# A sample's output projection and a router's logits on four column quarters of TensorE

## The reference

```python
def merge_branches(y_lru, o_nsa, ga, gb, w_proj_a, w_proj_b, w_out):
    return (sigmoid(ga) * (y_lru @ w_proj_a) + sigmoid(gb) * (o_nsa @ w_proj_b)) @ w_out

x = x + merge_branches(...)              # the residual
t = rms_norm(x, g_ffn)
logits = t @ router_w + router_b         # 1024 x 32
top_v, top_e = top_k(logits, 4)          # 4 of 32 experts for each row
gate = softmax(top_v)
# each expert: clamped SwiGLU of width 1024, its output weighted by gate and added to x
```

## Time and profile before

| | |
|---|---|
| three runs | 1765.46, 1769.73, 1770.02 us; median 1769.73 |
| profiled execution | 1770.05 us, its span 1768.40 us |
| TensorE's mean granted clock | 0.981 of full speed |
| busy in the span | PE 1694.9 us (96%), DVE 1137.3 (64%), ACT 886.6 (50%), POOL 220.2 (12%) |
| chain that ended last | PE 79%, DMA 11%, DVE 4%, issue 2%, ACT 2% |
| HBM | 488.10 MB read, 25.35 MB written, 290 GB/s over the span |

### The profile page before, as it was taken

How to read it: one execution, slowest core, us unless ns; L and a number is a source line. 1 busy time by engine, 2 the same in 40 slices (tenths; PEclk the granted TensorE clock), 3 DMA queues, 4 the chain that set the end, 5 groups by cost and what they waited for, 6 DMA issues and landing times.

```text
span 1768.4 us, 27559 instructions
## 1 busy us (share of the span) xinstructions
PE 1694.9 (96%) x10018; PEld 1312.8 (74%) x10018; DVE 1137.3 (64%) x1550; ACT 886.6 (50%) x1006; POOL 220.2 (12%) x262
## 2 busy tenths in 40 slices
PE   7999999999999999999989999999999999999998
PEld 4899978797776778777758675876768585876755
DVE  6766786645345756948668493848668493848661
ACT  5235645533322344737456472727466472727461
POOL 0022010003303123200100100100100100100100
PEclk9999999999999999999999999999999999999999
DMA  5063243114317617999999999999999999999995
GB/s 223 25 215 119 84 103 92 59 61 131 110 34 216 226 38 270 359 369 411 400 399 384 397 404 398 390 385 409 386 405 394 396 397 401 397 391 409 388 400 207
DMA packets 107795, 498.76 MB, mean 282 GB/s; under 512 B 20770, under 2 KB 41354, under 8 KB 57264
## 3 DMA queue, kind: packets, MB, share of 16 engines
q1 hardware_dynamic: 86592, 454.20, 65.5%
q0 software_dynamic: 20976, 42.93, 9.1%
q10 hardware_dynamic: 144, 0.55, 0.1%
HBM read 488.10 MB, written 25.35 MB: 290 GB/s over the span
## 4 chain that ended last, share of the span: by engine, by line
PE 79%; DMA 11%; DVE 4%; issue 2%; ACT 2%; SPq 0%; ACTq 0%; POOL 0%; DVEq 0%; POOLq 0%
PE bank L1247 23%; PE bank L1265 13%; DMA ring<-in_w_exp 10%; PE bank L751 7%; PE bank L803 5%; PE bank L651 5%; PE bank L1316 4%; PE bank L1301 3%; PE bank L678 3%; PE bank L1050 3%; PE bank L1025 1%; PE bank L837 1%; PE bank L816 1%; DMA slab<-in_w_tok 1%; PE bank L1218 1%
## 5 line engine op out<-in xcount | busy, mean ns | idle before, releaser
L2477 DVE TENSOR_TENSOR ring_rounded<-ring,wide_rounded 128x2048 fp32r<-128x2048 f32 x126 | 283.7, 2284 | 22.2 <-ACT wide_rounded L1719 22.1
L1719 ACT ACTIVATE wide_rounded<-ring 128x2048 fp32r<-128x2048 f32 x126 | 236.7, 1912 | 70.8 <-DMA ring<-in_w_exp 54.4
L1247 PE MATMUL bank<-ring_rounded,slab_rounded 128*128 128x512 f32 x672 | 261.7, 389 | 0.0
L2477 DVE TENSOR_TENSOR ring_rounded<-ring,xn_rounded 128x2048 fp32r<-128x2048 f32 x84 | 189.5, 2284 | 49.5 <-ACT xn_rounded L1719 49.1
L1247 PE MATMUL bank<-xn_rounded,slab_rounded 128*128 128x512 f32 x672 | 220.6, 399 | 0.0
L1719 ACT ACTIVATE xn_rounded<-ring 128x2048 fp32r<-128x2048 f32 x84 | 159.5, 1909 | 77.6 <-DMA ring<-in_w_exp 76.6
L1265 PE MATMUL bank<-wide_rounded,slab_rounded 128*128 128x512 f32 x504 | 170.6, 399 | 0.4 <-DVE slab_rounded L2571 0.3
L2617 DVE TENSOR_SCALAR slab<-bank 128x256 f32<-128x256 f32 x22 | 9.3, 425 | 238.0 <-PE bank L1301 238.0
L1247 PE MATMUL bank<-wide_rounded,slab_rounded 128*128 128x512 f32 x504 | 159.0, 390 | 0.0
L1301 PE MATMUL bank<-ring,slab 128*64 128x256 f32 x1408 | 156.2, 380 | 0.0
L751 PE MATMUL bank<-ring_rounded 128*128 128x260 f32 x768 | 149.4, 293 | 2.3 <-DVE slab_rounded L2092 2.3
(11 more groups left out here) (519 smaller groups left out, 3047.1 us busy)
## 6 DMA issues: line engine op xcount, KB each, us to landing
ring<-in_w_exp SPq DMA_DIRECT2D x384, 1024.0 KB, 12.8
ring<-in_w_blk SPq DMA_DIRECT2D x40, 512.0 KB, 3.7
slab<-in_w_tok SPq DMA_DIRECT2D x4, 1304.0 KB, 15.2
ring<-in_w SPq DMA_DIRECT2D x8, 512.0 KB, 3.2
ring<-in_w_out SPq DMA_DIRECT2D x2, 2048.0 KB, 14.9
xn<-in_xT SPq DMA_DIRECT2D x4, 520.0 KB, 8.2
ring<-in_k_cmp SPq DMA_DIRECT2D x32, 64.0 KB, 3.5
ring<-in_k_cmp POOLq DMA_DIRECT2D x32, 64.0 KB, 2.6
```

Of the source, the lines that this page charges most:

```text
L1247: r = mm(bank[:, c, :], a[:, 4 * h + k, :], w[:, k, :], start=False, stop=h == 1 and k == 3 and x == 2)
L1719: fn(WH[(2 * c + h) % 6], ring[:, half_of(c, h)], ACT.Copy).then_inc(S["wh_ready"], 1)
L2477: v.tensor_tensor(ring_r[:, half_of(c, h)], ring[:, half_of(c, h)], WHf[(2 * c + h) % 6], ALU.subtract)\
```

## The change

Tile 0's output projection is no longer three fp32r products of 512 columns, but f32: m's sample columns (a copy, `m_sample`, that ScalarE makes behind each high part) are stationary, 8 columns wide, and w_out, as WOH plus WOL, each read as f32, moves in four pieces of 256 columns, each written to its own 32 partitions of bank 3. These are 64 f32 calls for 48 fp32r matmuls. VectorE's residual of tile 0 goes in four pieces of 256 columns. The logits turn around: the router's 32 columns are stationary and the turned rows move, block pair j on partitions 32j to 32j + 31 of bank 3, 8 calls; ScalarE copies the 128 x 128 result (four partial sums, turned) to SBUF, and one f32 call with it as stationary operand and `stacked`, four unit matrices of 32 on top of each other, as moving operand adds the four and turns them back. That call stands in the middle of `out_part(t, 1, 0)`. VectorE builds `stacked` in three additions ahead of its preparation for the router. After the last tile, the second half of `first_expert(RT - 2)` moves between the two steps of the logits.

```diff
+        WOLf = [x.bitcast(F32) for x in WOL]
+        m_sample = kT_st[:, 1484:1484 + KD * NSA].rearrange("p (k n) -> p k n", k=KD)
+        logit_parts = oT_st[:, 1024:1024 + P]
+        stacked = oT_st[:, 1152:1152 + NE]
@@ tensor
-            def out_part(t, h, j):
+            def out_part(t, h, j, meanwhile=None):
                 n = tile_rows(t)[1]
-                if t == 0:
-                    pe.wait_ge(S["blk_lo"], NBLK + 8 + 2 * h + j + 1)
-                elif j == 0:
+                if t > 1 and j == 0:
                     pe.wait_ge(S["xm_ready"], 2 * t + h - 1)
                 for k in range(4 * j, 4 * j + 4):
-                    if t == 0 and h == 0:
+                    if t == 1 and h == 0:
                         pe.wait_ge(S["xw_lo"], 3 * KD + k + 1)
                     for x in range(3):
                         r = out_product(...)
+                    if meanwhile is not None and k == 4 * j + 1:
+                        logits(meanwhile)
+            def sample_rows():
+                for k in range(KD):
+                    pe.wait_ge(S["xw_hi"], 3 * KD + k + 1)
+                    for x in range(2):
+                        for j in range(4):
+                            h, a = j // 2, 256 * (j % 2)
+                            if k == 0 and a == 0:
+                                pe.wait_ge(S["blk_lo"], NBLK + 8 + 2 * h + 2)
+                            w = (WOHf, WOLf)[x][h].rearrange("p (k n) -> p k n", k=KD)
+                            r = mm(bank[32 * j:32 * j + NSA, 3, 0:256], m_sample[:, k, :], w[:, k, a:a + 256],
+                                   start=k == 0 and x == 0, stop=k == KD - 1 and x == 1)
+                            if k == KD - 1 and x == 1 and a:
+                                r.then_inc(S["wo_done"], 1)
...
+            def logits_by_expert(t):
+                n = tile_rows(t)[1]
+                pe.wait_ge(S["t_copied"], 3 * t + 2)
+                for x in range(2):
+                    for j in range(4):
+                        r = mm(bank[NE * j:NE * (j + 1), 3, 0:n], rwt[:, 2 * j + x, :], tT[:, 2 * j + x, 0:n], start=x == 0, stop=x == 1)
+                r.then_inc(S["lg_done"], 1)
+
             def logits(t):
                 n = tile_rows(t)[1]
-                pe.wait_ge(S["t_copied"], 2 * t + 2)
+                pe.wait_ge(S["t_copied"], 3 * t + 3)
...
-                for k in range(KD):
-                    r = mm(out, tT[:, k, 0:n], rwt[:, k, :], start=k == 0, stop=k == KD - 1)
-                r.then_inc(S["lg_done"], 1)
+                mm(out, logit_parts[:, 0:n], stacked, start=True, stop=True).then_inc(S["lg_done"], 1)
...
-            out_part(0, 0, 0)
-            out_part(0, 0, 1)
-            out_part(0, 1, 0)
-            out_part(0, 1, 1)
+            sample_rows()
             pe.wait_ge(S["m_ready"], 3 * KD)
             turn_part(0, 0)
...
-                logits(t - 1)
-                out_part(t, 1, 0)
+                logits_by_expert(t - 1)
+                out_part(t, 1, 0, t - 1)
...
             first_expert(RT - 2, range(0, 4))
+            logits_by_expert(RT - 1)
+            first_expert(RT - 2, range(4, KD))
             logits(RT - 1)
             places_before(RT - 1)
             places(RT - 1)
-            first_expert(RT - 2, range(4, KD))
             first_expert(RT - 1)
@@ scalar
             def merged_high(m):
                 act.wait_ge(S["m_ready"], 2 * KD + m + 1)
-                fn(MH[m], mT[:, m, :], ACT.Copy).then_inc(S["xw_hi"], 1)
+                fn(MH[m], mT[:, m, :], ACT.Copy)
+                fn(m_sample[:, m, :], mT[:, m, NPR:NT], ACT.Copy).then_inc(S["xw_hi"], 1)
...
+            def logits_copied(t):
+                n = tile_rows(t)[1]
+                act.wait_ge(S["lg_done"], 2 * t + 1)
+                fn(logit_parts[:, 0:n], bank[:, 3, 0:n], ACT.Copy).then_inc(S["t_copied"], 1)
...
             for t in range(RT):
                 if t >= 1:
                     turned_part(t - 1, 1)
+                    logits_copied(t - 1)
                 row_squares(t, 0)
@@ vector
             merged_low(KD - 1)
+            one(v.tensor_tensor(stacked, ident[:, 0:NE], ident[:, NE:2 * NE], ALU.add))
+            one(v.tensor_tensor(stacked, stacked, ident[:, 2 * NE:3 * NE], ALU.add))
+            one(v.tensor_tensor(stacked, stacked, ident[:, 3 * NE:4 * NE], ALU.add))
...
             def residual(t, h):
...
+                if t == 0:
+                    for j in (2 * h, 2 * h + 1):
+                        a = slice(256 * j, 256 * j + 256)
+                        one(v.scalar_tensor_tensor(xm[0:n, 0, a], bank[32 * j:32 * j + n, 3, 0:256], 0.5, xr[0:n, 0, a], ALU.mult, ALU.add),
+                            S["xm_ready"] if j % 2 else None)
+                    return
```

More of the change, by code:

```diff
@@ L1069, in turn_part @@
                 if t >= 1:
-                    pe.wait_ge(S["t_copied"], 2 * t + h - 1)
+                    pe.wait_ge(S["t_copied"], 3 * t + h - 2)
                 for k in range(4):
@@ L1691, in turned_part @@
                 if t >= 1:
-                    act.wait_ge(S["lg_done"], t)
+                    act.wait_ge(S["lg_done"], 2 * t - 1)
                 fn(tT[:, 4 * h:4 * h + 4, 0:n], bank[:, 2 + h, :].rearrange("p (k t) -> p k t", k=4)[:, :, 0:n], ACT.Copy)\
                     .then_inc(S["t_copied"], 1)
+            def logits_copied(t):
+                n = tile_rows(t)[1]
+                act.wait_ge(S["lg_done"], 2 * t + 1)
+                fn(logit_parts[:, 0:n], bank[:, 3, 0:n], ACT.Copy).then_inc(S["t_copied"], 1)
             def row_squares(t, h):
@@ L1748, in _ @@
                     high_half(0, 0, t - 2)
+            logits_copied(RT - 1)
             act.wait_ge(S["t_ready"], RT)
@@ L1848, in pair @@
                 block_of(n + 1, 1, "few", after_few=True)
-            act.wait_ge(S["lg_done"], RT)
+            act.wait_ge(S["lg_done"], 2 * RT)
             turned_rows(0)
@@ L2412, in choose @@
                 N = slice(0, n)
-                dve.wait_ge(S["lg_done"], t + 1)
+                dve.wait_ge(S["lg_done"], 2 * t + 2)
                 out = bank[N, 0, 0:NE] if t == RT - 1 else bank[N, 4, t * NE:(t + 1) * NE]
@@ L2492, in expert_order @@
             def expert_order():
-                dve.wait_ge(S["lg_done"], RT + 1)
+                dve.wait_ge(S["lg_done"], 2 * RT + 1)
                 one(v.tensor_copy(order_col.bitcast(I32), bank[0:NE, 7, 96:97]), S["oh_ready"])
@@ L2507, in sorted_slots @@
             def sorted_slots():
-                dve.wait_ge(S["lg_done"], RT + 2)
+                dve.wait_ge(S["lg_done"], 2 * RT + 2)
                 one(v.tensor_copy(entall[:, 2:NE, 0].bitcast(I32), bank[:, 0, 2:NE]))
```

## The result

The changed kernel takes 1769.36 us (median of 20 runs, 1766.31 to 1772.92); the kernel before, run beside it, 1766.67 us (20 runs, 1763.27 to 1770.60). The ratio is 1.0016, 95% interval 1.0008 to 1.0023. The predicted time of 1769.1 us and its range hold, and the difference is within 0.3%, as forecast with 0.83. But the sign of my sum does not hold: I summed to 0.6 us less and it is 2.7 us more, outside what the measurement leaves open. That the time itself came within 0.3 us is luck: I started from 1769.73 us, the median of three runs, and 20 runs put the kernel before at 1766.67. From there the forecast would have been 1766.1 us, 3.3 too low; a base 3.1 us too high made up for it. The profiled execution took 1772.31 us (span 1770.7) at a mean granted clock of 0.978. (Of early_again, further down, one execution took 3435.8 us; it is left out of that ratio, range and clock.)

The account below looks back on a forecast made before the run. The prediction took the experts' weight stream from HBM as the bound, with router-stage time reaching the end; plus 0.8 (tile 0), minus 0.8 (router) and minus 0.6 (last tile) gave minus 0.6 us: 1769.1 us, range 1764.0 to 1773.0.

Parts of the forecast that it names:

- the sign of my sum: Whole kernel: the terms were summed to 0.6 us less time, so a slightly faster kernel.
- what bounds tile 0: Tile 0: the residual waits behind VectorE's bias preparation, so shortening the projection from 11.09 to 6.9 us buys TensorE idle time.
- What the edit adds to VectorE: Tile 0: additions for `stacked`, split residuals and ScalarE's copy delay the chain, plus 0.8 us.
- the rivals with quarters that don't overlap: Tile 0's projection: no overlap, 27.6 us, total 1786.3, chance 0.03; only two overlap, 13.8 us, total 1772.5, chance 0.05.
- the one in which everything arrives: Rival: all saved TensorE time reaches the end, 8.1 us, total 1761.6, chance 0.12.
- the router: Logits of tiles 1 to 3: shorter products, partly lost to a wait for VectorE; net 0.26 us each, minus 0.8 us.
- tile 0's logits lie in VectorE's shadow: Router, tile 0: the logits are hidden behind VectorE's work before and after the change.
- the term for the clock behind the gap: After TensorE's idle 4.6 us in tile 0: a half-clock spell costing 0 to 1.8 us, taken as 0.
- after the last tile: Half of tile 3's picking product, 8 of 24 records, moves out of the way of tile 4's: minus 0.6 us.

Follow-up runs that it names:

- early_again: The changed kernel with tile 0's residuals moved ahead of the second bias step on VectorE, second run: 1766.51 us; kernel before there 1767.09.
- vector_added: The kernel before plus only ScalarE's copies, the three additions for `stacked` and tile 0's residual in pieces: 1767.66 us; kernel before there 1767.42.
- filler: The changed kernel with 18 products without use between tile 0's projection and its first turn: 1767.70 us; repeated on another chip, 1770.63 us.
- early_residual: The changed kernel with tile 0's residuals moved ahead of the second bias step on VectorE, first run: 1766.83 us; kernel before there 1767.07.
- sample_only: The kernel before with only tile 0's projection, ScalarE's copies and the residual in four pieces changed: 1768.61 us; kernel before there 1767.07.
- sample_again: The kernel before with only tile 0's part of the change, second run on another chip: 1768.67 us; kernel before there 1767.09.
- router_only: The changed kernel with tile 0's projection as it was, keeping the new logits and the order after the last tile: 1766.71 us; kernel before there 1767.07.
- router_again: The changed kernel with tile 0's projection as it was, second run on another chip: 1767.23 us; kernel before there 1767.09.
- short_tile0: The kernel before with 16 instead of 48 products in tile 0's projection, low products left out: 1768.37 us; kernel before there 1767.42.
- short_again: The kernel before with 16 instead of 48 products in tile 0's projection, second run: 1770.41 us; kernel before there 1767.09.
- old_order: The changed kernel with the second half of `first_expert(RT - 2)` put back after the last tile: 1765.04 us; kernel before there 1767.21.

## Why the prediction was right or wrong

**Right: what bounds tile 0.** Forecast: the four quarters run beside each other, 6.9 us (7.09 measured), VectorE reaches the residual behind the bias preparation, TensorE idles 4.6 us (4.50). All of the saved 4.0 us went there. What the edit adds to VectorE moved gates 0 by 0.5 us (vector_added), or 0.35 (filler, 26.74 beside 26.39), where I had 0.8. Neither of the rivals with quarters that don't overlap happened, and the one in which everything arrives did not either. early_residual shows the reason from the other side: with the residual ahead of the bias step it did wait for the projection, and the first turn came 3.4 us sooner.

**Right, nearly: the router.** Forecast 0.66 and 0.21 us for the two products (0.58 and 0.13), a stall of 0.57 (0.43), a gain of 0.26 a tile. From the logits' first record to `places_before` it is 4.89 us before (653.00 - 648.11) and 4.50 after (651.91 - 647.41), 0.39 less. From gates 1 to gates 3, with no half clock in either trace, the distance fell from 35.41 to 34.85 us, that is 0.28 a tile; from gates 0 to gates 3, at equal spells, by the 0.8 us of the forecast. One sentence here failed, that tile 0's logits lie in VectorE's shadow: with the spell, VectorE waited 1.36 us for them (L1108). In filler, without it, VectorE did not wait.

**Wrong: the term for the clock behind the gap.** The step was: "Such a spell would cost 0 to 1.8 us; part would hide [...] I take 0 and keep 1.8 for the range". All three profiles of the changed kernel have the spell, 6.8, 6.8 and 3.4 us long, and the slack that I counted on was not enough: TensorE, ahead of VectorE in tile 1 before, became the later one by 0.79 and 1.36 us. By gates 0, against the filler, which has no spell there, the short spell costs 0.8 us and the long one 1.3 to 1.7, where I had 0. The timed runs agree: the sample part alone is 1.5 and 1.6 us above the kernel before, with a smaller addition to VectorE than the whole change has. The row for this was in hand: the earlier trace rows has twelve matmuls at half clock behind an idle stretch. I read it as a risk, when it was the nearest row to what the edit makes. (That row was also no matter of idle time alone: TensorE had stood 0.35 us and then worked 3.9 us on products of eight rows.) The Trainium skill ("TensorE: Matmul & The Clock Gate", Part 1) has idleness bring the 1.2 GHz level, and here the traces agree: 3.8 to 4.5 us of idle time (sample_only, sample_again, changed) were followed by products 0.39 to 0.43 us apart.

**Wrong: after the last tile.** The step was "I take minus 0.6 us". I priced the records that go out of the way and not what the new step puts in: a product that waits for ScalarE, on whose answer the choice, the places and so the picking product depend. From gates 3 to the first expert, with the copy on time, the new order takes 13.15 to 13.20 us (filler, both early residuals), 13.39 and 13.67 (router_only, router_again), where the kernels with the old logits take 13.29 to 13.39. So no gain is shown where I had 0.6: the 16 records of the picking product then wait 0.83 us for VectorE's positions, and went at 0.21 us each (3.41 us in the filler), half rate. With the copy late, as in all three profiles of the changed kernel, it is a loss of 1.9 to 2.7 us. With tile 0's 1.5 us and the router's 0.8 back, these would come to 2.6 to 3.4 us, and the result is 2.7; but that sum takes the copy to be late in the timed runs too, which is not shown. With the copy on time it would be some 0.6 to 1.1 us. What is sure of the sign is that the gain that I put at 0.6 did not come and that tile 0 cost more than the router gave.

**The same account by the clock.** Over the 20 timed runs of the changed kernel the time falls by 0.96 us for every 0.001 of mean granted clock (correlation -0.82). Its mean is 0.9803, later 0.9794 and 0.9808, where the kernel before has 0.9823 to 0.9830: 1.5 to 3 us. On the fitted line at a clock of 0.981 the changed kernel is at 1769.1 to 1769.7 us, the kernel before at 1768.3 to 1768.9. So for the changed kernel more of the slip goes with the clock than is left at equal clock (under 1.5 us). This is a correlation, and the mean clock is that of the whole kernel: of the 78.2 us at half clock in the changed kernel's profile only 22.7 lie in the router stage. Nor does the clock decide alone: early_residual, at 0.9800, is as fast as the kernel before at 0.9830.

**Open.** What holds ScalarE's copy is not settled. It was late in 7 of the 12 profiled executions of kernels that have both parts, and in neither of the two with the router's part alone. In none of the seven late ones does a packet of an instruction queue fall into the wait, so the trace does not show a fetch. The cause of the chip-to-chip answers is open too. No kernel with the copy taken off ScalarE was tried.

## What to carry to other kernels

Before shortening an engine's work, look at what stands in the queue of the engine that takes the result over: if that is busy with something else, the saving becomes idle time, and here idle time on TensorE was followed by half-clock products that cost 0.8 to 1.7 us. Move the other engine's work first (here the residual ahead of the bias step, worth some 2.5 us), then shorten. Before comparing a stage in two profiles, look at the granted clock in both: a spell of half clock that one of them drew by chance was worth 1.6 us here, more than any term of my sum. And when a few microseconds in 1770 are at stake, compare the mean granted clock of many runs beside their times, and run a variant on two chips before believing it: two of my clearest answers fell on the second.

## What the runs showed of the hardware that I had not expected

- Products in f32 with eight stationary columns on four quarters overlap four-wide: 128 records of 256 columns in 7.09 us, 0.055 us each. On two column halves the same kind of record cost 0.108.
- A kernel that does 32 products less, ahead of a place where TensorE must wait anyhow, is slower by 1 to 3.3 us (short_tile0, short_again).
- The clock also fell without idle time to speak of: in the kernel before at 640.7 us, behind 3.9 us of products of eight rows and 0.35 us of idle time.
- The kernel before answered with 1766.7 to 1767.4 us on every chip, while variants of it that differ in a few instructions moved by 3 to 4 us between two chips (filler, old_order), in the profiles each time with the late copy. None of the causes is known.
- The Trainium skill ("TensorEngine Tiling (Array Packing)", Key Properties) has a change of the tiling mode drain TensorE. The trace is in keeping with it, and puts a bound on it: 16 router records on quarters take 0.58 us from their start to the next product, where 16 / 4 x 0.107 would be 0.43. The 0.15 us between them is an estimate of all that getting in and out costs; the trace does not tell a drain from the rest.
